# A causal ConvFFN's first GEMM on one Trainium2 core: two neighbouring pairs by seven block products between plain ones, instead of one and one

## The reference, cut to what matters

```python
def conv_ffn(hn, w_up, conv_w, conv_b, w_down):      # D_MODEL 1024, D_FF 2816, 3 taps
    u = causal_dwconv(hn @ w_up, conv_w, conv_b)
    gate, val = u[..., :D_FF], u[..., D_FF:]
    return (jax.nn.silu(gate) * val) @ w_down
```

## Time and profile before

| | |
|---|---|
| median of 3 runs | 2525.95 us (2525.37 to 2526.32) |
| the profiled execution's own time | 2525.95 us |
| its span, first to last instruction | 2524.2 us |
| mean granted TensorE clock | 0.992 |
| busy, share of the span: TensorE | 2470.5 us, 98% |
| VectorE | 1615.6 us, 64% |
| ScalarE | 1155.4 us, 46% |
| GpSimd | 602.3 us, 24% |
| seven pairs and the plain pairs between them, layer 0 | 937.46 to 1234.54 us |
| the same, layer 1 | from 1986.98 us |

### The profile page before, as it was taken

One profiled execution on the slowest core, in us unless ns is written; L12 is line 12 of the kernel. 1 busy time (PEld: TensorE's weight loads), 2 busy tenths in 40 slices (PEclk: granted clock), 3 DMA queues, 4 the chain that ended last, 5 costly groups with the idle time before them and its releaser, 6 DMA issues.

```text
span 2524.2 us, 45974 instructions
## 1 busy us (share of the span) xinstructions
PE 2470.5 (98%) x18254; PEld 1724.5 (68%) x18254; DVE 1615.6 (64%) x2424; ACT 1155.4 (46%) x2166; POOL 602.3 (24%) x417
## 2 busy tenths in 40 slices
PE   8999999999999999999999999899999999999998
PEld 5566666666665667777766666676656777777665
DVE  6676777787868887777511276594379777772123
ACT  5455655666415554444311255595355444441111
POOL 1002113122142122232122113264411223221221
PEclk9999999999999999999999999999999999999999
DMA  3132222323132111212311112100121121213111
GB/s 118 54 104 79 85 84 80 97 68 99 45 127 101 51 51 50 65 35 66 126 46 58 40 34 68 34 2 18 43 110 50 51 66 34 66 56 126 46 57 67
DMA packets 67808, 167.69 MB, mean 66 GB/s; under 512 B 5680, under 2 KB 37840, under 8 KB 67408
## 3 DMA queue, kind: packets, MB, share of 16 engines
q1 hardware_dynamic: 67664, 165.70, 19.8%
HBM read 151.76 MB, written 12.86 MB: 65 GB/s over the span
## 4 chain that ended last, share of the span: by engine, by line
PE 86%; DVE 8%; ACT 3%; ACTq 1%; POOL 1%; issue 1%; DVEq 1%; DMA 0%
PE PS L2260 22%; PE PS L2262 22%; PE PS L2261 22%; PE PS L2661 4%; PE PS L2659 4%; PE PS L2660 4%; PE PS L2536 1%; PE PS L2543 1%; DVE BIG L1629 1%; PE PS L2525 1%; DVE TT L1693 1%; POOL BIG L869 1%; PE PS L2354 1%; ACT BIG L1539 1%; DVE R L460 1%
## 5 line engine op out<-in xcount | busy, mean ns | idle before, releaser
L2260 PE MATMUL PS<-R,whi 128*128 128x384 f16 (+2 forms) x2400 | 747.4, 311 | 2.6 <-DVE wlo L1594 1.6
L2262 PE MATMUL PS<-R,wlo 128*128 128x384 f16 (+2 forms) x2400 | 747.2, 311 | 0.0
L2261 PE MATMUL PS<-R,whi 128*128 128x384 f16 (+2 forms) x2400 | 747.1, 311 | 0.0
L1594 DVE SCALAR_TENSOR_TENSOR wlo<-stage,whi 128x1024 f16<-128x1024 f32 (+1 forms) x148 | 204.5, 1383 | 380.7 <-ACT whi L884 379.9
L2260 PE MATMUL PS<-BIG,whi 128*128 128x384 f16 (+2 forms) x1404 | 435.4, 310 | 4.9 <-DVE wlo L1594 4.2
L2262 PE MATMUL PS<-BIG,wlo 128*128 128x384 f16 (+2 forms) x1404 | 435.4, 310 | 0.0
L2261 PE MATMUL PS<-BIG,whi 128*128 128x384 f16 (+2 forms) x1404 | 435.3, 310 | 0.0
L2260 PEld LDWEIGHTS PS<-R,whi 128*128 128x128 f16 x2400 | 235.3, 98 | 127.7 <-issue 14.2
L2261 PEld LDWEIGHTS PS<-R,whi 128*128 128x128 f16 x2400 | 235.4, 98 | 121.3 <-issue 9.8
L2262 PEld LDWEIGHTS PS<-R,wlo 128*128 128x128 f16 x2400 | 235.4, 98 | 118.0 <-issue 1.0
L884 ACT ACTIVATE whi<-stage 128x1024 f16<-128x1024 f32 (+1 forms) x148 | 162.5, 1111 | 148.3 <-PE PS L2262 128.5
(11 more groups left out here) (285 smaller groups left out, 4556.7 us busy)
## 6 DMA issues: line engine op xcount, KB each, us to landing
stage<-wa SPq DMA_DIRECT2D x164, 512.0 KB, 3.5
stage<-wd SPq DMA_DIRECT2D x32, 704.0 KB, 4.0
TT<-cs_rows SPq DMA_DIRECT2D x32, 512.0 KB, 3.7
h_keep<-hT SPq DMA_DIRECT2D x2, 4160.0 KB, 12.4
EC<-cs_rows SPq DMA_DIRECT2D x64, 128.0 KB, 3.7
hT<-h SPq DMA_DIRECT2D x4, 1536.0 KB, 10.6
hT<-h_keep SPq DMA_DIRECT2D x4, 1536.0 KB, 8.5
out<-hT SPq DMA_DIRECT2D x4, 768.0 KB, 3.5
```

The costliest lines, as they stand in the source:

```text
L1594: eng.scalar_tensor_tensor(out=WL[d][:, 0:width], in0=stage[:, slot, 0:width], scalar=WS, in1=WH[d][:, 0:width], op0=ALU.mult, op1=ALU.sub ...
L2260: eng.matmul(acc, WH[slot][:, ws], xh, start=first, stop=False)
L2261: eng.matmul(acc, WH[slot][:, ws], xl, start=False, stop=False)
L2262: return eng.matmul(acc, WL[slot][:, ws], xh, start=False, stop=last)
```

## The change

**Order.** Pairs 0 to 6 plain, 7 seven, then four rounds (NR) of one plain pair and two seven pairs (RS = 2): 8 plain, 9 and 10 seven, 11 plain, 12 and 13 seven, 14 plain, 15 and 16, 17 plain, 18 and 19; then 20 plain and 21 seven. That makes ten seven pairs a layer instead of eight, twelve plain ones instead of fourteen.

**Operands.** The first seven pair's operands are split during the plain pair, as before. The second's are split during the first seven pair: ScalarE's `op_high` waits for the product that read the operand's buffer (`beside`), VectorE's `op_low` stands between its adds (`ops`). The seven operands are now made in the order in which TensorE uses them, and GpSimd makes three of the four weight sums ahead of `hidden_lo` instead of two, with a second scratch tile, `tmp2`.

**First product.** `seven_first` holds the two copies of the first product. In front of the second seven pair it stands behind `gate` and ahead of `hidden` of the first one; elsewhere behind `hidden` of the pair before, as it did.

**Banks.** A seven pair behind a seven pair waits for VectorE's adds (`seven_v`) where it waited for ScalarE's evacuation (`evac`), and for all 14 of them before its seventh partial product.

The two weight units of the plain pair behind are split in the second seven pair of a round (`split_next`, `lo_next`); they can be loaded once `op_low` of S4 has released `stage`, at the end of the first seven pair.

```diff
 SF = 7
-NS = (KF - SF + 1) // 2
+RS = 2
+RP = RS + 1
+NR = (KF - SF - 3) // RP
+NS = 2 + RS * NR
...
-A11, A12, A22, S1, S3, S2, S4 = range(7)
+A11, S2, A12, S3, S1, A22, S4 = range(7)
+FIRST, REST = (A11, S2, A12, S3), (S1, A22, S4)
...
-        tmp = BIG[:, 21, 0:HP]
+        tmp, tmp2 = BIG[:, 21, 0:HP], BIG[:, 21, HP:2 * HP]
...
@@ GpSimd, weight_sums @@
                 if n > 0:
-                    eng.wait_ge(op_lo, m * 7 + (7 * (n - 1) + 6))
+                    eng.wait_ge(op_lo, m * (7 * RS) + 7 * n)
                 eng.tensor_tensor(tmp, a21, a22, ALU.add).then_inc(op_sum, 1)
                 eng.drain()
+                eng.tensor_tensor(tmp2, tmp, a11, ALU.subtract).then_inc(op_sum, 1)
                 eng.tensor_tensor(a21, a11, a21, ALU.subtract).then_inc(op_sum, 1)
+                eng.drain()
                 before()
-                eng.wait_ge(op_lo, m * 7 + (7 * n + 4))
-                eng.tensor_tensor(tmp, tmp, a11, ALU.subtract).then_inc(op_sum, 1)
-                eng.drain()
-                eng.tensor_tensor(a12, a12, tmp, ALU.subtract).then_inc(op_sum, 1)
+                eng.wait_ge(op_lo, m * (7 * RS) + (7 * n + A12 + 1))
+                eng.tensor_tensor(a12, a12, tmp2, ALU.subtract).then_inc(op_sum, 1)
...
@@ ScalarE @@
+            def op_high(layer, m, i, n, o, beside):
...
+                if beside:
+                    eng.wait_ge(seven, m * (14 * RS) + (14 * (n - 1) + 2 * o + 2))
...
+            def seven_first(layer, m, i, n, c0):
+
+                n, i_ = NS * layer + n, m * RP + i
+                eng.wait_ge(conv[1], i_ + c0)
                 for q in range(2):
...
+                    eng.wait_ge(seven, m * (14 * RS) + (14 * n + 1 + q))
                     eng.activation(up_out(layer, 1, q, False), PS[:, q, 0:piece(layer, q)[1]], ACT.Copy,
                                    scale=1.0 / WS).then_inc(seven_a, 1)
...
+            def seven_pair(layer, m, i, n, c0, gate, hidden, behind_seven=False, split_next=None, op_next=None):
+
+                if not behind_seven:
+                    seven_first(layer, m, i, n, c0)
+                n0, n, i_ = n, NS * layer + n, m * RP + i
+                if split_next is not None:
+                    split_next(0)
+                    split_next(1)
+                if op_next is not None:
+                    for o in FIRST + REST[:-1]:
+                        op_next(o)
                 eng.drain()
...
+                eng.wait_ge(seven_v, m * (14 * RS) + (14 * n + 12))
+                up_tap(layer, m, i, 0)
+                if op_next is not None:
+                    op_next(S4)
                 eng.drain()
...
+                eng.wait_ge(seven_v, m * (14 * RS) + (14 * n + 14))
+                up_tap(layer, m, i, 1)
                 eng.drain()
                 eng.sem_inc(evac, 6)
-                gate(i)
-                hidden(i)
+                gate(i_)
+                if op_next is not None:
+                    seven_first(layer, m, i + 1, n0 + 1, c0)
+                hidden(i_)
...
@@ VectorE, seven_pair (add() as before) @@
+                def ops(*os):
+                    if op_next is not None:
+                        for o in os:
+                            op_next(o)
...
                 eng.drain()
                 for q in range(2):
                     add(4, q, c11[q], c11[q])
-                lo_next(0)
+                if lo_next is not None:
+                    lo_next(0)
+                ops(A11, S2)
                 for q in range(2):
                     add(6, q, u3[q], u2[q])
-                lo_next(1)
+                if lo_next is not None:
+                    lo_next(1)
+                ops(A12, S3)
                 for q in range(2):
                     add(8, q, u4[q], u2[q])
+                ops(S1)
                 eng.drain()
                 for q in range(2):
                     add(10, q, c21[q], u3[q])
                     eng.drain()
                     add(8, q, c22[q], u3[q])
+                ops(A22)
                 add(12, 0, c12[0], u4[0])
...
+                up_taps(layer, m, i, n0, 0, (0,))
+                up_taps(layer, m, i, n0, 1, (1, 0))
+                ops(S4)
+                product(m * RP + i)
...
@@ VectorE, ffn_up (ScalarE, GpSimd and TensorE loop in the same order) @@
-                last_plain(0, 0)
-                with eng.Fori(0, NS - 1) as m:
-                    seven_pair(layer, m, 0, product, lambda s_: split_lo(m * 4 + (u0 + 2 * SF + 3 + s_), s_))
-                    last_plain(m, 1)
-                seven_pair(layer, 0, NS - 1, product, lambda s_: lo(U_DN[layer] + s_, KU * P))
...
+                last_plain(0, SF - 1, 0, SF - 1)
+                seven_pair(layer, 0, SF, 0, product, lo_plain(0, SF + 1))
+                with eng.Fori(0, NR) as m:
+                    last_plain(m, SF + 1, 1, SF)
+                    for j in range(RS - 1):
+                        seven_pair(layer, m, SF + 2 + j, 1 + j, product, op_next=lambda o: op_low(layer, m, 2 + j, o))
+                    seven_pair(layer, m, SF + RP, RS, product, lo_plain(m, SF + RP + 1))
+                last_plain(0, KF - 2, NS - 1, KF - NS - 1)
+                seven_pair(layer, 0, KF - 1, NS - 1, product, lambda s_: lo(U_DN[layer] + s_, KU * P))
...
@@ TensorE, seven_pair @@
+                def free(bank):
+                    if behind_seven:
+                        eng.wait_ge(seven_v, m * (14 * RS) + (14 * (n - 1) + (6, 10, 12, 12, 12, 13)[bank]))
+                    else:
+                        eng.wait_ge(evac, m * (6 * RP) + (kept + bank + 1))
...
+                if behind_seven:
+                    eng.wait_ge(seven_v, m * (14 * RS) + 14 * n)
                 multiply(6, 0, S3, turn(T_3))
```

More of the change, by code:

```diff
@@ L242, in program, with landed @@
         OPS = halves_of(AUXh, 0, 14)
-        tmp = BIG[:, 21, 0:HP]
+        tmp, tmp2 = BIG[:, 21, 0:HP], BIG[:, 21, HP:2 * HP]
         def op_src(o):
-            return (stage[:, 1, 0:HP], stage[:, 1, HP:2 * HP], stage[:, 0, HP:2 * HP], tmp, stage[:, 0, 0:HP], tmp,
+            return (stage[:, 1, 0:HP], tmp2, stage[:, 1, HP:2 * HP], stage[:, 0, 0:HP], tmp, stage[:, 0, HP:2 * HP],
                     stage[:, 1, HP:2 * HP])[o]
+        def landed(layer, m, i):
+            return m * (16 * RP) + 16 * ((U_UP[layer] + 2 * i) // 2 + 1)
         T_ROW = (8, 10, 17, 19)
@@ L1358, in op_high, with up_tap @@
                     eng.sem_inc(w_hi, 2)
-            def up_tap(layer, m, i0, s_):
-                col = m * 16 + (C_F[layer] + 8 * (SF + 2 * i0) + 4 * s_)
+            def up_tap(layer, m, i, s_):
+                col = m * (8 * RP) + (C_F[layer] + 8 * i + 4 * s_)
                 a = LO_DN[layer]
@@ L2045, in up_taps, with seven_pair @@
                     r.then_inc(conv[s_], 1)
-            def seven_pair(layer, m, i0, product, lo_next):
-                n, i = NS * layer + i0, m * 2 + (SF + 2 * i0)
+            def seven_pair(layer, m, i, n, product, lo_next=None, op_next=None):
+                n0, n = n, NS * layer + n
                 def add(e, q, dst, term):
-                    eng.wait_ge(seven, m * 14 + (14 * n + e + q + 1))
+                    eng.wait_ge(seven, m * (14 * RS) + (14 * n + e + q + 1))
                     eng.scalar_tensor_tensor(out=dst, in0=PS[:, (e + q) % 7, 0:piece(layer, q)[1]],
@@ L2696, in ffn_up @@
                         tile(i * 2 + (U_UP[layer] + 4 + s_), i * 6 + 3 * (J_UP[layer] + 4 + s_), s_, s_, x_r1, LO_UP[layer])
-                with eng.Fori(0, NS - 1) as m:
-                    seven_pair(layer, m, 0)
+                seven_pair(layer, 0, SF, 0)
+                with eng.Fori(0, NR) as m:
                     for s_ in range(2):
-                        after_seven(layer, m, s_)
-                seven_pair(layer, 0, NS - 1)
+                        after_seven(layer, m, SF + 1, 0, s_)
+                    for j in range(RS):
+                        seven_pair(layer, m, SF + 2 + j, 1 + j, j > 0)
+                for s_ in range(2):
+                    after_seven(layer, 0, KF - 2, NS - 2, s_)
+                seven_pair(layer, 0, KF - 1, NS - 1)
             def kv_free(pos):
```

151 lines of the change are left out of this document (74 added, 77 removed).

## The result

The changed kernel takes 2531.5 us against 2526.2 us in the same sessions (medians of 16 runs each): ratio 1.0021, 95% interval 1.0014 to 1.0029. It is 5.2 us slower; 2536 was predicted. Its profiled execution has a span of 2530.0 us and took 2532.1 us.

The account below looks back on a forecast made before the run. TensorE bounds the kernel now; after the change the VectorE/ScalarE chain with GpSimd collisions would. Waits of 20.4 us less 10.1 saved give +10.3 on 2525.95: 2536 us, 0.4% slower, range 2522 to 2548.

Parts of the forecast that it names:

- the first rival: Both layers' rounds: TensorE stays the bound, only 5 us of GpSimd's work collide, no waits, 2515.9 us; chance 0.13.
- TensorE's saving: Two pairs a layer from plain to seven: 2.54 us each in layer 0, 2.49 in layer 1, 10.1 us in all.
- landing and split: Plain pair's first unit after `stage` is released: 3.9 us landing, 1.0 ScalarE's split, 0.3 handovers, 5.2 us together.
- the walk: VectorE's and ScalarE's new order through one round: 53.4 us bare, 61.1 with 7.7 us of GpSimd collisions (layer 1: 60.8).
- The sum: Four rounds in each layer: waits 9.6 + 10.8 = 20.4 us, less 10.1 saved, +10.3, giving 2536 us.
- The deficit: TensorE's wait per round: 61.1 - 58.4 = 2.7 us in layer 0, 60.8 - 57.8 = 3.0 in layer 1.
- The single seven pair behind the rounds: After the last round of a layer: it waits as the first of a round does, the first round hardly.
- The slack of 1.2 us: Before the eighth partial product: copy needed 9.4 us into a pair, before ended 8.0 us in; used up once per layer.
- Parts at nothing: Operand order, `tmp2`, `seven_v` bank waits and the copy ahead of `hidden`: said to cost nothing.
- The copy's place: Second seven pair's first-product copy: left behind `hidden`, it would come another 2.5 us later.
- TensorE stays the bound: Rival for the rounds: chain under 59.4 us, TensorE remains the bound and is faster, 2515.9 us; chance 0.13.
- The clock falls: Rival at TensorE's fourteen waits of 1 to 2 us: clock falls to 1.2 GHz, 18 us more, 2554 us; chance 0.03.

Follow-up runs that it names:

- e4_sum_before_hidden_lo: Changed kernel with GpSimd making S4's weight sum ahead of the plain pair's `hidden_lo` instead of behind it: 2517.9 us, ratio 0.9967 to the kernel before.
- e3_one_and_one: Changed kernel with RS = 1, one seven pair to each plain one again, all else of the change kept: 2525.1 us, ratio 0.9997 to the kernel before.
- e5_lo_behind_adds: Changed kernel with VectorE's `lo` of the plain pair behind the eight adds of the first products: 2523.6 us, ratio 0.9990 to the kernel before.
- e1_sums_narrow: Changed kernel with weight sums S3 and S4 made on only 32 of 512 columns (computation left out): 2518.2 us, ratio 0.9966 to the kernel before.
- e7_copy_late_sums_first: Changed kernel with the first product's copy behind `hidden` and S4's sum ahead of `hidden_lo`: 2525.1 us, ratio 0.9998 to the kernel before.
- e8_three_in_a_row: RS = 3, on the changed kernel with S4's sum ahead of `hidden_lo` and `lo` behind the adds: 2537.3 us, ratio 1.0049 to the kernel before.
- e6_both: Changed kernel with S4's sum ahead of `hidden_lo` and the plain pair's `lo` behind the adds: 2518.1 us, ratio 0.9967 to the kernel before.
- e2_copy_behind_hidden: Changed kernel with the second seven pair's first-product copy put back behind `hidden`: 2545.5 us, ratio 1.0078 to the kernel before.

## Why the prediction was right, and where its size was off

**Direction and mechanism: right.** The chain of VectorE and ScalarE over a round is the bound, TensorE waits at the one place named, and the collisions of VectorE with GpSimd decide between faster and slower: with two sums made small, or one moved, the same instructions of the other engines give no or hardly any waits, and the first rival's 2515.9 us (TensorE the bound) is nearly reached, at 2517.9. TensorE waits nowhere else, so the bank waits put at nothing were nothing. The margin was small: by the prediction's own sum the change comes out even at a deficit of 1.6 us a round, and 2.05 was measured. The change of +5.2 us is half of the +10.3 forecast.

**TensorE's saving** is right: 18.62 and 21.15 us a pair stand in the changed kernel, and in `e4_sum_before_hidden_lo` the two stretches are 5.1 and 5.0 us shorter than before, as forecast. That its time is only 8 us shorter is due to what lies outside them (see Open).

**The chain, part by part** (predicted bare and with its collisions, measured from 1106.89 to 1167.34):

| part | predicted | measured |
|---|---|---|
| first seven pair to the end of S4's `op_low` | 16.4 + 3.05 = 19.45 | 19.33 |
| landing and split, to `lo_next(0)` | 5.2 | 4.73 |
| second seven pair to the end of the product | 14.9 + 2.1 = 17.0 | 17.03 |
| to the plain pair's first `op_low` | 1.8 | 1.77 |
| four `op_low`, two taps | 5.4 + 2.55 = 7.95 | 7.93 |
| silu, copies, tap | 3.9 | 3.77 |
| taps and product | 4.2 | 4.26 |
| hidden, copy, first add | 1.6 | 1.63 |
| sum | 61.1 | 60.45 |

The collisions fell where the walk had put them: A11's `op_low` 1.13 - 0.68 = 0.45 us longer (predicted 0.65), S2's `op_low` 2.64 - 0.68 = 1.96 (predicted 2.0), S1's 1.08 - 0.68 = 0.4, the plain pair's first 2.43 as before, the tap beside the fourth sum 1.89 - 1.30 = 0.6 (0.85), and three taps beside the next sums 0.43, 0.74 and 0.76 (0.5, 0.8, 0.8). One was not placed: `lo_next(0)` took 1.50 us for 1.21, begun beside a `hidden_lo` (1129.21 to 1131.37). In sum 7.4 us where 7.7 was predicted.

**What was mis-sized: the step "The sum", 20.4 us of waits where 13.6 were measured.** Two terms of it:
- *The deficit, 2.7 us a round*, is 2.05 (in layer 1 about 2.3 for 3.0), above all by the landing and split, 5.2 against 4.73. ScalarE began on the unit 1129.87 - 1126.22 = 3.65 us after S4's `op_low` had ended, where the 3.9 of the earlier trace rows and a handover make 4.05. One landing was read and taken for all: of the first units of a pair in the kernel before, loaded between 1016 and 1108 us, it is the longest (3.3 to 3.9 us), and this one took 3.4. In the eight rounds 8 x 0.65 = 5.2 us.
- *The single seven pair behind the rounds* was said to wait "as the first of a round does". Those wait 1.28 us (layer 1: 1.58), it waits 0.49 (0.69). The plain pair ahead of it is written out behind the loop, and there the way from its first `op_low` to the copy takes 16.29 us where it takes 17.07 in a round. That is 0.8 us less in layer 0 and 0.9 in layer 1.

```profile
1166.82 0.65 ACT L1385 ACTIVATE UB<-PS 128x272 f32<-128x272 f32 x2
...
1210.19 2.24 DVE L2060 SCALAR_TENSOR_TENSOR AUX<-stage,AUX 128x512 f16<-128x512 f32 x1 [1.76 <-ACT AUX L1368]
...
1226.48 0.64 ACT L1385 ACTIVATE UB<-PS 128x272 f32<-128x272 f32 x2
```

Together that is 5.2 + 0.8 + 0.9 = 6.9 us, where forecast and measurement differ by 6.8. The slack of 1.2 us was right: 4 x 2.05 - 0.79 - 1.2 gives 6.2, the waits of layer 0. That the forecast is only 4.5 us above the result is luck: some 2 us outside the two stretches go the other way and were not foreseen.

The split within a round, 0.9 in the second seven pair and 1.2 to 2 in the first, measured 0.76 and 1.28 (layer 1: 0.72 and 1.58); "none in the first round" measured 0 in the first double pair. VectorE's idleness in front of `lo_next(0)`, said to be 2 to 3 us, was 1.55.

**Parts at nothing** held (`e3_one_and_one`). **The copy's place**, put at 2.5 us a time if left behind `hidden`, came out at 2.5 to 2.8 us of wait, and cost 14 us in the sum: half of it longer waits, half the clock.

**Rivals.** "TensorE stays the bound" needed a chain under 59.4 us; the changed kernel's 60.45 was one sum's place away from it. "The clock falls" did not happen in the changed kernel's two stretches (clock 1.00 in each of their windows above, waits up to 1.58 us), but its refutation was weak: the prediction leaned on 1524 to 1540 us, idle 4.5 us at clock 1.00, and the same stretch of the changed kernel, idle 3.6 us, has 0.89. One execution in which the clock held is no evidence that it holds. And outside the two stretches the clock did fall more than before, as told next.

**Open.** One thing is the time that the kernels with `RS = 2` or 3 lose outside the two stretches. 0.4 us of it is outside the span: time less span is 2.05 to 2.25 us in all their executions, 1.65 to 1.77 in those of the kernel before and of `e3_one_and_one`. The rest goes with TensorE's clock. From the last seven pair of layer 0 to the first of layer 1 the kernel before takes 771.1 us, 17 of them at 1.2 GHz. `e5_lo_behind_adds` and `e1_sums_narrow` take 771.5 and 771.9 with 20 us of it, `e7_copy_late_sums_first` and `e8_three_in_a_row` 772.1 and 772.3 with 24, the changed kernel (less the pair's own wait), `e4_sum_before_hidden_lo`, `e6_both` and `e2_copy_behind_hidden` 772.7 to 773.3 with 27. In the changed kernel one such stretch stands at 1534 to 1538 us (granted clock 0.57, before 1.00): its matmuls fall 1.6 us behind those of the kernel before and win back 1.0 at the wait behind it. These are single executions; over all executions the mean clock is 0.9914 in the changed kernel (16) and 0.9926 in the kernel before (46). What brings the slow clock there, in stages that the change leaves alone, was not tried; another offset of these stages against each other is a guess. Why four of the eight waits of 2.5 to 2.8 us brought the slow clock and four did not is open too; the longest, 2.82, did not.

## What to carry to other kernels

When an engine's slack is what separates two loads of the bound engine, add up the chain of the others over the new round before removing it, with the collisions of VectorE and GpSimd as terms of their own; it is paid in each of eight rounds here, and 1.24 us less idleness a round took 8.5 us of waits away (`e5_lo_behind_adds`). An instruction of GpSimd that is not urgent belongs beside work of VectorE that reads PSUM: moving a sum of 1.65 us ahead of a `hidden_lo` of 2.2 turned 0.2% slower into 0.3% faster. Then stop: a second edit of the same kind was worth nothing, and with one more load in a row the waits grew to 25.5 us, by the trace for a single staging buffer above all.

## What the runs showed of the hardware that was not expected

- A wait of TensorE of 2.5 to 2.8 us between dense matmuls brought the clock to 1.2 GHz for 3.4 us in four cases of eight, at a price of 1.6 to 1.7 us each; each time the slow clock began within 0.5 us of the wait's end. In the stretches of the changed kernel 14 waits of up to 1.58 us, and in `e7_copy_late_sums_first` eight of up to 1.33 us, brought it in none.
- The exclusion of VectorE and GpSimd lengthens both: GpSimd's sums took 2.10 and 2.28 us (1141.09, 1143.13) beside taps, 1.28 alone, and `hidden_lo` took 2.61 where it began beside S1's `op_low` (1109.71 in `e4_sum_before_hidden_lo`) and 2.16 where it began first. A product of two float32 tiles on VectorE, 1.24 us alone, took 2.11 at 1098.35 in `e1_sums_narrow`, where a sum of GpSimd (1098.08, 1.28 us) had begun before it; in the changed kernel the product came first (1104.02) and kept its 1.24, and the sum took 2.08. The Trainium skill, "SBUF — State Buffer", section "Who interferes with whom", says that the one that was issued first keeps the other waiting, whichever engine it is on; the trace agrees.
